# One PSUM bank pair instead of two, and the shared attention loop, in the memory cross-attention

## The reference

```
x = layer_norm(DN_ALPHA * x + mixer(x), ...)            # ln0
q = (x @ w_q);  k, v = (mem @ w_kv)                     # 4 heads of 64
s = einsum('bqhd,bmhd->bhqm', q, k) * 64 ** -0.5
p = softmax(s)
y = einsum('bhqm,bmhd->bqhd', p, v).reshape(B, S, 256) @ w_o
x = layer_norm(DN_ALPHA * x + y, ...)                   # ln1
y = square(relu(x @ mlp_w_up)) @ mlp_w_down             # the MLP, then ln2
```

## Time and profile before

| | |
|---|---|
| median of 3 runs | 1766.67 us (1766.26 to 1769.02) |
| profiled execution, its own time | 1769.02 us |
| its span in the profile | 1767.2 us |
| mean granted TensorE clock | 0.974 of full |
| PE busy / DVE / ACT / POOL | 94% / 57% / 40% / 38% of the span |

### The profile page before, as it was taken

One profiled execution on the slowest core, in us unless ns is written; L12 is line 12 of the kernel. 1 busy time (PEld: TensorE's weight loads), 2 busy tenths in 40 slices (PEclk: granted clock), 3 DMA queues, 4 the chain that ended last, 5 costly groups with the idle time before them and its releaser, 6 DMA issues.

```text
span 1767.2 us, 34126 instructions
## 1 busy us (share of the span) xinstructions
PE 1662.8 (94%) x15054; PEld 1527.0 (86%) x15054; DVE 1000.9 (57%) x1602; ACT 712.8 (40%) x1099; POOL 671.3 (38%) x539
## 2 busy tenths in 40 slices
PE   7999999899999999998999879999999799999997
PEld 7878988899979888987999778999998698999985
DVE  3255466777763354476777766663345567653245
ACT  3444544544445444444444444532223344332222
POOL 0644673000307635743000313425647406154546
PEclk9999999899999999998999979999999899999999
DMA  7422345777545323464775444533223444432322
GB/s 286 173 96 96 120 146 204 269 281 264 176 159 208 120 73 115 136 264 191 268 275 204 171 143 144 180 120 121 97 97 120 143 156 136 150 121 97 121 85 95
DMA packets 44147, 283.55 MB, mean 160 GB/s; under 512 B 5160, under 2 KB 5288, under 8 KB 14176
## 3 DMA queue, kind: packets, MB, share of 16 engines
q1 hardware_dynamic: 42336, 272.23, 43.6%
q0 software_dynamic: 1664, 9.15, 1.4%
HBM read 280.30 MB, written 1.06 MB: 159 GB/s over the span
## 4 chain that ended last, share of the span: by engine, by line
PE 80%; DVE 7%; POOL 6%; ACT 4%; issue 2%; DMA 0%; DVEq 0%; POOLq 0%; SPq 0%; ACTq 0%
PE ps L532 78%; PE ps L540 3%; POOL part0l L2667 2%; POOL part1l L2667 2%; ACT part1h L2226 1%; ACT part0h L2226 1%; DVE Xl L1278 1%; DVE gates L1966 1%; DVE part1l L1263 1%; DVE part0l L1263 0%; ACT Xh L2226 0%; DMA hid<-in_xT 0%; ACT gates L2223 0%; POOL x L2702 0%; ACT Z L2223 0%
## 5 line engine op out<-in xcount | busy, mean ns | idle before, releaser
L532 PE MATMUL ps<-Xh,part0h 128*128 128x256 f32 x1080 | 320.8, 297 | 9.7 <-DVE Xl L1278 7.9
L2226 ACT ACTIVATE part0h<-ring 128x1024 fp32r<-128x1024 f32 (+2 forms) x218 | 216.3, 1041 | 272.4 <-PE ps L532 265.4
L2667 POOL TENSOR_TENSOR part1l<-ring,part1h 128x512 fp32r<-128x512 f32 x194 | 254.0, 1341 | 159.6 <-ACT part1h L2226 159.6
L532 PE MATMUL ps<-Xl,part0h 128*128 128x256 f32 x1080 | 312.7, 290 | 0.0
L532 PE MATMUL ps<-Xh,part0l 128*128 128x256 f32 x1080 | 312.4, 289 | 0.0
L2226 ACT ACTIVATE part1h<-ring 128x1024 fp32r<-128x1024 f32 x218 | 216.2, 1040 | 235.1 <-PE ps L532 234.2
L2667 POOL TENSOR_TENSOR part0l<-ring,part0h 128x512 fp32r<-128x512 f32 x184 | 245.0, 1364 | 170.4 <-ACT part0h L2226 170.3
L532 PE MATMUL ps<-Xh,part1h 128*128 128x256 f32 x984 | 286.8, 291 | 5.9 <-DVE Xl L1278 4.1
L532 PE MATMUL ps<-Xl,part1h 128*128 128x256 f32 x984 | 280.0, 285 | 0.0
L532 PE MATMUL ps<-Xh,part1l 128*128 128x256 f32 x984 | 279.8, 284 | 0.0
L532 PEld LDWEIGHTS ps<-Xh,part0h 128*128 128x128 f32 x1080 | 214.6, 199 | 19.1 <-DVE Xl L1278 9.6
(11 more groups left out here) (409 smaller groups left out, 3284.6 us busy)
## 6 DMA issues: line engine op xcount, KB each, us to landing
ring<-in_w SPq DMA_DIRECT2D x214, 1024.0 KB, 5.0
hid<-in_ada SPq DMA_DIRECT2D x36, 512.0 KB, 6.5
hid<-in_w SPq DMA_DIRECT2D x6, 1024.0 KB, 10.7
rows<-in_lnrow POOLq DMA_DIRECT2D x6, 1024.0 KB, 7.0
fqk<-in_ada SPq DMA_DIRECT2D x6, 512.0 KB, 6.7
cq<-in_ada SPq DMA_DIRECT2D x6, 512.0 KB, 5.9
gates<-in_c SPq DMA_DIRECT2D x2, 1536.0 KB, 7.5
plain<-in_w SPq DMA_DIRECT2D x2, 1024.0 KB, 7.0
```

The lines of the kernel that those rows point to most:

```text
L532: return e.matmul(o, a, b, start=st, stop=sp)
L2226: return e.activation(o, a, ACT.Copy)
L2667: e.tensor_tensor(lo[:, o], raw[:, o], f32(hi[:, o]), ALU.subtract).then_inc(*G("low", m, h))
```

## The change

Every attention now uses one pair of banks, 6-7. `Psum` keeps it as `self.beside`, and `reserve`, `release`, `take_pair` and `pair` lose their lists. The cross-attention is done by the shared `attention(l, "x")` on PE, DVE and ACT, with a list of jobs for its six steps; `cross_out(i)` now issues both halves of the columns. The rest of the diff takes the job names into `job1`.

```diff
-    def reserve(self, *first):
-        self.beside = list(first)
-        for b in first:
+    def reserve(self):
+        for b in self.beside:
             self.order.remove(b)
-            self.order.remove(b + 1)
...
     def take_pair(self, w, kind, *name):
-        b = self.beside.pop(0)
-        self.beside.append(b)
-        return [self.hold(w, b + j, (kind, j, *name)) for j in range(2)]
+        return [self.hold(w, b, (kind, j, *name)) for j, b in enumerate(self.beside)]
...
+             "x": "|xv0 xv1|||xOT0 up0|xo0"}
...
@@ tensor_program, cross
-        u = attention_units("x")
-        ps.reserve(4, 6)
-        scores(l, u[0])
-        scores(l, u[1])
-        memory_values(l, 0)
-        for k in range(2):
-            turn_weights(l, u[k])
-            scores(l, u[2 + k])
-        memory_values(l, 1)
-        turn_weights(l, u[2])
-        weigh(l, u[0])
-        weigh(l, u[1])
-        turn_weights(l, u[3])
-        turn_cross(l, 0)
-        weigh(l, u[2])
-        weigh(l, u[3])
-        ps.release()
-        cross_out(l, 0, 0)
+        attention(l, "x")
         turn_cross(l, 1)
-        cross_out(l, 0, 1)
-        for ch in range(2):
-            cross_out(l, 1, ch)
+        cross_out(l, 1)
...
@@ vector_program, job1 and cross
+        elif name in ("xv0", "xv1"):
+            values_out(l, int(name[2]))
+        elif name == "up0":
+            split_to(PIECE[l, "up0"])
+        elif name == "xOT0":
+            turned_cross(l, 0)
+        elif name == "xo0":
+            for ch in range(2):
+                residual(l, "xo", 0, ch)
+            variance(l, 1, 0)
...
-        u = attention_units("x")
-        soften(l, u[0])
-        soften(l, u[1])
-        split_to(PIECE[l, "up0"])
-        values_out(l, 0)
-        turned_weights(l, u[0])
-        soften(l, u[2])
-        soften(l, u[3])
-        values_out(l, 1)
-        turned_weights(l, u[2])
-        close(l, u[1])
-        turned_cross(l, 0)
-        close(l, u[3])
+        attention(l, "x")
         turned_cross(l, 1)
+        normalize(l, 1, 0)
         for ch in range(2):
-            residual(l, "xo", 0, ch)
-        variance(l, 1, 0)
-        residual(l, "xo", 1, 0)
-        normalize(l, 1, 0)
-        residual(l, "xo", 1, 1)
+            residual(l, "xo", 1, ch)
...
@@ scalar_program, cross
-        split_to(PIECE[l, "up0"])
-        u = attention_units("x")
-        for k in range(3):
-            exponentials(l, u[k])
-        turned_weights(l, u[1])
-        exponentials(l, u[3])
-        turned_cross(l, 0)
-        turned_weights(l, u[3])
+        attention(l, "x")
         turned_cross(l, 1)
```

More of the change, by code:

```diff
@@ L163, in __init__ @@
         self.all, self.tiles, self.where, self.freed = banks, [banks[:, b, :] for b in range(8)], {}, {}
+        self.beside = [6, 7]
         self.restart()
@@ L180, in take, with pair @@
         return self.hold(w, b, name)
-    def reserve(self, *first):
-        self.beside = list(first)
-        for b in first:
+    def reserve(self):
+        for b in self.beside:
             self.order.remove(b)
-            self.order.remove(b + 1)
     def release(self):
-        self.order += [b + j for b in self.beside for j in range(2)]
+        self.order += self.beside
     def take_pair(self, w, kind, *name):
-        b = self.beside.pop(0)
-        self.beside.append(b)
-        return [self.hold(w, b + j, (kind, j, *name)) for j in range(2)]
-    def pair(self, kind, *name):
-        b = self.where.get((kind, 0, *name), 0)
-        return self.all[:, b:b + 2, :]
+        return [self.hold(w, b, (kind, j, *name)) for j, b in enumerate(self.beside)]
+    def pair(self):
+        return self.all[:, self.beside[0]:self.beside[1] + 1, :]
     def give(self, *name):
@@ L441, in fills @@
                   "g0_3.0 cs1|g0_3.1 cT1|g1_0.0 cv0|g1_0.1 cv1|g1_1.0|g1_1.1|g1_2.0|g1_2.1",
-             "m": "g1_3.0 g1_3.1|g2_0.0 g2_0.1 OT0|g2_1.0 g2_1.1 OT1|g2_2.0 g2_2.1|OT3 g2_3.0|g2_3.1"}
+             "m": "g1_3.0 g1_3.1|g2_0.0 g2_0.1 OT0|g2_1.0 g2_1.1 OT1|g2_2.0 g2_2.1|OT3 g2_3.0|g2_3.1",
+             "x": "|xv0 xv1|||xOT0 up0|xo0"}
     out = {kind: [s.split() for s in text.split("|")] for kind, text in steps.items()}
@@ L692, in attention @@
         between = Jobs(fills(l).get(kind, ()), lambda name: job1(l, name))
-        ps.reserve(6)
+        ps.reserve()
         for t in range(len(units) + 2):
@@ L762, in job1 @@
             turn_out(l, 2 * int(name[2]))
+        elif name in ("xv0", "xv1"):
+            memory_values(l, int(name[2]))
+        elif name[0:3] == "xOT":
+            turn_cross(l, int(name[3]))
+        elif name[0:2] == "xo":
+            cross_out(l, int(name[2]))
         elif name == "kc":
@@ L921, in turn_cross, with cross_out @@
         last.then_inc(*P("xOT", i, l))
-    def cross_out(l, i, ch):
+    def cross_out(l, i):
         hl = [v(h, k=2, c=1024) for h in weights(l, "xo")]
         w.wait_ge(*at["xOT", i, l])
[L926 to L931, removed]
+        for ch in range(2):
+            t = ps.take(w, "xo", i, ch, l)
+            for k in range(2):
+                low_half(l, "xo", k, 2)
+                last = mm3(t[:, :], [h[:, k, i * 128:(i + 1) * 128] for h in M.A1],
+                           [h[:, k, ch * 512:(ch + 1) * 512] for h in hl], k == 0, k == 1)
+            last.then_inc(*P("xo", i, ch, l))
     def mlp(l):
@@ L1390, in soften @@
         nk = key_tiles(u) * 128
-        b = (ps.pair("qk", u, l) if beside(u) else v(ps["qk", u, l][:, :], j=2, k=256))[:, :, 0:nk]
+        b = (ps.pair() if beside(u) else v(ps["qk", u, l][:, :], j=2, k=256))[:, :, 0:nk]
         if u[0] == "x":
```

## The result

The changed kernel takes **1787.41 us** (median of 4 runs, 1785.43 to 1788.94) against 1766.47 us for the kernel before (4 runs, 1765.56 to 1769.02). The ratio is 1.0115, with a 95% interval of 1.0098 to 1.0133: it is slower by about 21 us, where 16.5 were forecast.

The account below looks back on a forecast made before the run. PE, busy for 94% of the span, with an MLP run without waits that passes on any delay, was taken as the bound. 2 x (8.75 - 0.5) = 16.5 us, counted from 1766.67, gave 1783.2 us; range 1775 to 1790.

Parts of the forecast that it names:

- The direction and the chain: Cross-attention stage: slower; scores of u1 2.08 us late, `turn_cross(1)` 7.69, last residual 6.45 at full clock, 8.75 with slow `cross_out(1)`.
- the memory values: PE, behind the new wait of u1's scores: 3.56 us each, as before, covering u1's softmax.
- the clock falls earlier: Rival: clock falls from 308 to 317, slowing `cross_out(0)` and transposes too; 3 us more per layer, 1789.2; chance 0.08.
- The clock in `cross_out(1)`: After a 4.4 us gap on PE, its matmuls run at 1.2 GHz: 2.3 us more per layer, bounds 0 and 2.3.
- The 0.5 us "taken back" per layer: Allowance for the clock rising elsewhere around the MLP's slow start: 0.5 us per layer, bounds 0 to 3.
- The second pair was worth nothing: Rival: other work covers u1's wait for the shared banks, so 2 x 2.08 falls away: 1779.0; chance 0.06.
- The MLP takes the delay up: Rival: MLP matmuls wait for weights that could run ahead, so those waits shrink, not slower: 1766.7; chance 0.04.
- POOL and SP: Queues moved past: POOL's rows ready at 306.6 before `close(u1)` at 311, SP's later `up3` load covered; cost nothing.
- a gap of 3.6 to 4.4 us: PE's idle before the clock falls: 3.6 us in the kernel before, 4.4 expected ahead of `cross_out(1)`.

Follow-up runs that it names:

- e1: Changed kernel with two pairs of banks (4-5 and 6-7) given back to the cross-attention, job order as changed: 1778.9 us, ratio 1.0072.
- e3: Changed kernel with DVE's residuals of the first 128 tokens put back behind the second turned output, so `close` of u3 comes first: 1779.0 us, ratio 1.0076.
- e2: Changed kernel with the split of `up0` listed in step 1, beside the memory values, instead of step 4: 1782.9 us, ratio 1.0090.
- e6: Changed kernel with two pairs, `up0` split early and `close` before the first residuals, all together: 1772.2 us, ratio 1.0036.
- e5: Changed kernel, still one pair, with the first memory values between the scores of u0 and u1: 1778.9 us, ratio 1.0068.
- e4: Kernel before, in its hand-written order, with only one pair of banks (6-7): 1775.9 us, ratio 1.0057.
- e9: Kernel before with one pair and PE and DVE reordered, other work in front of each scores that needs the pair again: 1768.2 us, ratio 1.0014.
- e8: Changed kernel with idle matmuls, results unread, in PE's waits (four after u0's scores, six after u3's weighing, one before `cross_out(1)`): 1778.1 us, ratio 1.0061.

## Why the prediction was right, and which term was too small

*The direction and the chain* were right. Counted from the first scores of the first layer: scores of u1 at 2.62 forecast, 2.63 measured; from `turn_cross(0)` to the end of `up0`'s subtractions 4.15 and 4.20; from `turn_cross(0)` to `turn_cross(1)` 8.59 and 8.55; from there to the last residual 6.69 and 6.55. The last agrees in part by luck: the clock came back before the last three matmuls, so that from the first matmul of `cross_out(1)` to the last residual it took 4.93 instead of 5.35, while the slow transposes ahead of them took 0.3 more than reckoned. e1 to e3 took each suspect away: the waits shrank as forecast in both layers, the stages within 0.9 us of the forecast except in the second layer of e2 and e3, which came out 3.0 and 2.3 us shorter because the clock was full there. e6 left the forecast rest.

*The term that failed is the memory values*: "Then the memory values take 3.56 each". I put them behind the new wait at their old speed. The clock fell there, at about 300.7 us, behind two waits of 0.78 and 1.93 with only the scores between, and they took 8.69 and, in the second layer, 9.28 us (811.52 to 820.80) instead of 7.12: 1.6 and 2.2 us, and in the second layer the scores of u1 0.5 more. So the last residual came 10.33 and 11.33 us later than before relative to the first scores, not 8.75. That is 4.2 us in all, the size of the 4.4 by which 16.5 was short of 20.9. The two are not proved to be the same microseconds: in the two profiled executions the MLP runs and the rest of the kernel gave 4.5 back, and their whole difference was 16.4. The rival "the clock falls earlier" looked for the fall from 308 on, behind the memory values instead of ahead of them, and judged it by gaps of 0.35. Its 1789.2 is nearer to 1787.4 than the forecast is, but by luck: `cross_out(0)`, which it had slow, ran at the full clock.

*The clock in `cross_out(1)`* at half was right in both layers for the first matmuls (nine and eight of twelve). In the changed kernel and in e5 the clock fell in the wait of 3.0 us before `turn_cross(1)`, in e1 in that wait in the first layer and just behind it in the second; in e3, with 0.53, it did not fall. With waits between (1.94 in e2, 0.53 and 1.62 in e6) it fell in the first layer and not in the second. The 0.5 us "taken back" per layer was too little: the second transposes take 1.09 instead of 1.97, which makes the stage 0.4 shorter, and the MLP runs are 177.92 and 177.83 us instead of 179.20 and 179.25, 1.3 and 1.4 shorter. Of the first, 0.8 was lost again before the second layer's scores.

*"The second pair was worth nothing"* was wrong for both orders tried with the scores in their place (e1, e4). Once other work covers the waits, one pair came near to two (e5, e9), though neither of these orders was run with two pairs. The case of the Trainium skill in which double-buffering gave no further gain ("TensorE: Matmul & The Clock Gate", "HAM oscillation — how this bites in real kernels") is approached here only by e5, whose time with one pair equals that of e1 with two; e4 speaks against taking it as a rule.

*"The MLP takes the delay up"* was wrong: its run has no wait to give back, 177.92 us in one piece. POOL and SP did as said: POOL's rows were done before `close`, and no matmul waited for `up3`.

What stays open is where exactly the clock falls in later stages; it was not controlled here. Runs of one kernel lie 1.8 us (e5) to 7.3 us (e3) apart; in e3 the mean granted clock was 0.978 in the fastest and 0.972 in the slowest. Open is also why the clock stayed full in the second layer of e3 behind the same two waits.

## What to carry to other kernels

When a buffer is halved, write down what stands in the waiting engine's queue right behind the wait; if independent work can be put in front instead, the single buffer cost little here (e9: 0.14%; e5: no more than two pairs in the uncovered order), and if not, it costs the wait and the slow matmuls behind it (e4). In a shared loop, look at which jobs come ahead of the instruction that another engine waits for: three microseconds of residuals ahead of one `close` cost 2.8 to 2.9 us a layer here (e3), more than the missing banks' first wait of 1.9. Price every new wait on PE twice, once as time and once as clock.

## What the runs showed of the hardware

- The granted clock fell after far less idle time than the prediction reckoned with (a gap of 3.6 to 4.4 us): behind waits of 0.78 and 1.93 us with 0.6 us of scores between in the changed kernel, in e2, in the first layer of e3, and in e4, where the second wait was 2.10; in the second layer of e3 it did not fall behind the same waits. Where idle matmuls of 2.0 us filled the second wait, the memory values took 7.17 us in both layers (e8).
- DVE's two subtractions of 1024 columns and POOL's additions slow each other: 4.44 us and 2.25 when they overlap, 2.36 and 1.26 when apart. Each of the two slowed subtractions took 2.23 or 2.29 us, nearly as long as one of each engine's together (1.22 and 1.26), as if the engines took turns; that is an inference from these durations. POOL's timeline before and after:

```profile
299.56 2.25 POOL L2702 TENSOR_TENSOR x<-xh,rows 128x512 f32<-128x512 f32 x1
```
```profile
299.64 1.26 POOL L2679 TENSOR_TENSOR x<-xh,rows 128x512 f32<-128x512 f32 x1
```
